# Decoder trunk with GLA, sliding-window attention and product-key experts: the gate one-hots unrolled over all tiles, one sub-key search in every query unit, two splits moved ahead of two pair subtractions

## The reference, cut to what matters

```python
def peer_ffn(h, wq, subkeys, u, v):
    K = PEER_TOPK                                        # 16
    q = (h @ wq).reshape(B, T, PEER_HEADS, 2, PEER_QDIM // 2)
    s = einsum('bthpd,pnd->bthpn', q, subkeys)           # 8 heads x 2 halves, 128 sub-keys each
    s_top, i_top = lax.top_k(s, K)
    cand = s_top[..., 0, :, None] + s_top[..., 1, None, :]
    cand_idx = i_top[..., 0, :, None] * PEER_NKEYS + i_top[..., 1, None, :]
    best, pos = lax.top_k(cand.reshape(B, T, PEER_HEADS, K * K), K)
    experts = take_along_axis(cand_idx.reshape(B, T, PEER_HEADS, K * K), pos, axis=-1)
    gates = softmax(best)
    a = einsum('td,tkd->tk', h, u[experts])              # u, v: 16384 x 1024
    return einsum('tk,tkd->td', gates * gelu(a), v[experts])
```

## Time and profile before

| | |
|---|---|
| median of three executions | 4135.0 us (4130.0 to 4140.92) |
| the profiled execution | 4135.81 us, its span 4134.0 us, mean granted PE clock 0.977 |
| PE | 3918.7 us busy (95%), 18074 matmuls |
| PE weight loads | 3171.5 us (77%) |
| DVE | 2835.7 us (69%) |
| POOL | 1833.8 us (44%) |
| ACT | 1534.9 us (37%) |

### The profile page before, as it was taken

One profiled execution on the slowest core, in us unless ns is written; L12 is line 12 of the kernel. 1 busy time (PEld: TensorE's weight loads), 2 busy tenths in 40 slices (PEclk: granted clock), 3 DMA queues, 4 the chain that ended last, 5 costly groups with the idle time before them and its releaser, 6 DMA issues.

```text
span 4134.0 us, 49995 instructions
## 1 busy us (share of the span) xinstructions
PE 3918.7 (95%) x18074; PEld 3171.5 (77%) x18074; DVE 2835.7 (69%) x4368; ACT 1534.9 (37%) x2262; POOL 1833.8 (44%) x956
## 2 busy tenths in 40 slices
PE   6899989989999999999988999899899999999999
PEld 5667767877877887888876677688687878788887
DVE  6435535798898937888764364258898978378786
ACT  3436523333333333333334364233333333333332
POOL 2322233334444447677423223334443444477772
PEclk9999999999999999999999999999999999999999
DMA  8744593333544469999857455633344445799995
GB/s 311 250 158 160 187 356 119 108 124 127 198 174 158 170 223 369 367 354 352 303 192 244 161 191 187 213 121 131 122 154 170 170 162 193 265 367 367 355 353 204
DMA packets 411796, 918.88 MB, mean 222 GB/s; under 512 B 38352, under 2 KB 176464, under 8 KB 409968
## 3 DMA queue, kind: packets, MB, share of 16 engines
q1 hardware_dynamic: 327600, 664.77, 46.4%
q0 software_dynamic: 45056, 134.38, 8.9%
q10 hardware_dynamic: 38976, 117.66, 7.3%
HBM read 794.00 MB, written 256.90 MB: 254 GB/s over the span
## 4 chain that ended last, share of the span: by engine, by line
PE 76%; issue 8%; DVE 5%; DMA 4%; POOL 4%; ACT 3%; SPq 0%; POOLq 0%; ACTq 0%; DVEq 0%
PE ps L942 13%; PE ps L943 13%; PE ps L944 13%; PE ps L957 10%; PE ps L958 10%; PE ps L959 10%; POOL w_lo L896 4%; DMA raw<-in_stream_dram 4%; PE ps L1253 2%; ACT w_hi L554 1%; PE ps L1143 1%; DVE raw L1329 1%; DMA ada_first<-in_stream_dram 0%; DVE hot_i L1686 0%; PE ps L1094 0%
## 5 line engine op out<-in xcount | busy, mean ns | idle before, releaser
L896 POOL TENSOR_TENSOR w_lo<-raw,w_hi 128x1024 fp32r<-128x1024 f32 x440 | 1124.3, 2556 | 1938.6 <-ACT w_hi L554 1938.3
L554 ACT ACTIVATE w_hi<-raw 128x1024 fp32r<-128x1024 f32 x504 | 534.0, 1060 | 1774.9 <-PE ps L944 1307.3
L942 PE MATMUL ps<-h_hi,w_hi 128*128 128x512 f32 x2880 | 1139.5, 396 | 18.1 <-POOL w_lo L896 9.6
L943 PE MATMUL ps<-h_hi,w_lo 128*128 128x512 f32 x2880 | 1131.0, 393 | 0.0
L944 PE MATMUL ps<-h_lo,w_hi 128*128 128x512 f32 x2880 | 1130.0, 392 | 0.0
L942 PEld LDWEIGHTS ps<-h_hi,w_hi 128*128 128x128 f32 x2880 | 546.0, 190 | 142.3 <-issue 17.5
L944 PEld LDWEIGHTS ps<-h_lo,w_hi 128*128 128x128 f32 x2880 | 544.0, 189 | 118.5
L943 PEld LDWEIGHTS ps<-h_hi,w_lo 128*128 128x128 f32 x2880 | 544.8, 189 | 106.3
L909 POOL DMA_INDIRECT down<-expert_down,e_row x256 | 337.0, 1316 | 220.0 <-DVE ps L1739 94.5
L1686 DVE TENSOR_TENSOR hot_i<-same_i,pick 128x1024 fp32r<-128x1024 f32 x192 | 421.2, 2194 | 0.0
L901 POOL DMA_INDIRECT acts<-expert_act,e_act x256 | 372.2, 1454 | 103.9 <-issue 77.4
(11 more groups left out here) (255 smaller groups left out, 5796.4 us busy)
## 6 DMA issues: line engine op xcount, KB each, us to landing
raw<-in_stream_dram SPq DMA_DIRECT2D x648, 512.0 KB, 3.8
expert_down<-in_stream_dram SPq DMA_DIRECT2D x256, 512.0 KB, 5.9
expert_act<-gel ACTq DMA_DIRECT2D x256, 256.0 KB, 2.0
raw_more<-in_stream_dram SPq DMA_DIRECT2D x128, 512.0 KB, 6.6
expert_gate<-gatebuf ACTq DMA_DIRECT2D x12, 4096.0 KB, 12.4
a_in<-expert_act SPq DMA_DIRECT2D x128, 384.0 KB, 6.6
g_in<-expert_gate SPq DMA_DIRECT2D x128, 384.0 KB, 8.2
ada_first<-in_stream_dram SPq DMA_DIRECT2D x3, 2048.0 KB, 20.6
```

The costliest lines, as they stand in the source:

```text
L554: return act.activation(o, i, ACT.Copy)
L896: pool.tensor_tensor(w_lo[:, s, :], raw[:, b, :], w_hi[:, s, :].bitcast(F32), ALU.subtract).then_inc(lo_ready, 1)
L942: pe.matmul(o, w_hi[:, s, w], mov_hi[:, c, :], start=c == 0, stop=False)
L943: pe.matmul(o, w_lo[:, s, w], mov_hi[:, c, :], start=False, stop=False)
```

## The change

Three edits, all in the DVE stream. First, `sub_keys` is called behind `q_lo` of every query unit from the second on, so fifteen searches lie between the units and one after them. Second, the loop over three tiles is written out as 96 groups: the one-hots read `idxT` itself in place of the copy `pick`, and `add_lower` of a tile's last three groups comes three groups later, within the next tile's; semaphore counts are constants. Third, at the start of the down stage `split_down(0)` and `split_down(1)` come ahead of `pair_lo(2)` and `pair_lo(3)`. POOL's stream, which subtracts all lower halves outside the down stage, is the same as before, and so are PE's, ACT's and SP's.

```diff
--- before.py
+++ after.py
@@ -1588,7 +1588,7 @@
                     dve.wait_ge(qhi_ready, l * 16 + n + 1)
                     tt_op(q_lo[:, n % 2, :], ps[:, ORDER[m] % 2, :], q_hi[:, n % 2, :].bitcast(F32), ALU.subtract
                           ).then_inc(col_dve, 1)
-                    if n >= 3 and (n - 3) % 4 < 3:
+                    if n:
                         sub_keys(sides)
                         sides += 1
                 for n in range(sides, 16):
@@ -1667,49 +1667,45 @@
                 dve.wait_ge(idx_ready, (l + 1) * DT)
 
                 iota4 = iota.unsqueeze(1).to_broadcast([P, 4, P])
-                with dve.Fori(0, DT) as tt:
-                    step.enter(tt, 1)
-                    step(dve.tensor_copy(pick[:], idxT[:, bass.ds(tt + 1, 1)].rearrange("p o a b -> p (o a) b")))
-
-                    def row(n, r):
-                        return pick[:, r, 4 * n:4 * n + 4].unsqueeze(2).to_broadcast([P, 4, P])
-
-                    def one_hot(n):
-
-                        dve.wait_ge(hot_used, tt * 32 + (l * DT * 32 + n + 1))
-                        tt_op(hot_j[:, n % HOT], iota4, row(n, 1), ALU.is_equal)
-                        tt_op(same_i[:, n % 2], iota4, row(n, 0), ALU.is_equal).then_inc(same_ready, 1)
-
-                    def weigh(n):
-
-                        dve.wait_ge(same_ready, tt * 32 + (l * DT * 32 + n + 1))
-                        tt_op(hot_i[:, n % HOT], same_i[:, n % 2].unsqueeze(2).to_broadcast([P, 4, 2, P]),
-                              pick[:, 2:4, 4 * n:4 * n + 4].rearrange("p a t -> p t a").unsqueeze(3).to_broadcast([P, 4, 2, P]),
-                              ALU.mult).then_inc(hot_ready, 1)
-
-                    def add_lower(n):
-
-                        half, t = n // 16, 4 * (n % 16)
-                        dve.wait_ge(gate_upper, tt * 32 + (l * DT * 32 + n + 1))
-                        both = ps[:, 4 + n % 2 * 2:6 + n % 2 * 2, :].rearrange("p a (b i) -> p (a b) i", b=4)
-                        g4 = gatebuf[:, half, :, t:t + 4]
-                        tt_op(g4, both[:, 1:8:2, :].rearrange("p t i -> p i t"), g4, ALU.add).then_inc(gate_ready, 1)
-
-                    one_hot(0)
-                    for n in range(32):
-                        if n < 31:
-                            if n:
-                                dve.wait_ge(hot_ready, tt * 32 + (l * DT * 32 + n))
-                            one_hot(n + 1)
-                        weigh(n)
-                        if n >= 3:
-                            add_lower(n - 3)
-                    for n in range(29, 32):
-                        add_lower(n)
-                    dve.wait_ge(hot_ready, tt * 32 + (l * DT * 32 + 32))
-                step.leave(DT)
+
+                def row(n, r):
+                    return idxT[:, n // 32 + 1, r, n % 32 * 4:n % 32 * 4 + 4].unsqueeze(2).to_broadcast([P, 4, P])
+
+                def one_hot(n):
+
+                    dve.wait_ge(hot_used, l * DT * 32 + n + 1)
+                    tt_op(hot_j[:, n % HOT], iota4, row(n, 1), ALU.is_equal)
+                    tt_op(same_i[:, n % 2], iota4, row(n, 0), ALU.is_equal).then_inc(same_ready, 1)
+
+                def weigh(n):
+
+                    dve.wait_ge(same_ready, l * DT * 32 + n + 1)
+                    both_parts = idxT[:, n // 32 + 1, 2:4, n % 32 * 4:n % 32 * 4 + 4].rearrange("p a t -> p t a")
+                    tt_op(hot_i[:, n % HOT], same_i[:, n % 2].unsqueeze(2).to_broadcast([P, 4, 2, P]),
+                          both_parts.unsqueeze(3).to_broadcast([P, 4, 2, P]), ALU.mult).then_inc(hot_ready, 1)
+
+                def add_lower(n):
+
+                    half, t = n // 16 % 2, 4 * (n % 16)
+                    dve.wait_ge(gate_upper, l * DT * 32 + n + 1)
+                    both = ps[:, 4 + n % 2 * 2:6 + n % 2 * 2, :].rearrange("p a (b i) -> p (a b) i", b=4)
+                    g4 = gatebuf[:, half, :, t:t + 4]
+                    tt_op(g4, both[:, 1:8:2, :].rearrange("p t i -> p i t"), g4, ALU.add).then_inc(gate_ready, 1)
+
+                one_hot(0)
+                for n in range(DT * 32):
+                    if n < DT * 32 - 1:
+                        if n:
+                            dve.wait_ge(hot_ready, l * DT * 32 + n)
+                        one_hot(n + 1)
+                    weigh(n)
+                    if n >= 3:
+                        add_lower(n - 3)
+                add_lower(DT * 32 - 3)
+                add_lower(DT * 32 - 2)
+                add_lower(DT * 32 - 1)
+                dve.wait_ge(hot_ready, (l + 1) * DT * 32)
                 pick_tile(0)
-
                 def product(j):
                     b = j % 4
                     dve.wait_ge(ag_loaded[b], 32 * (l * 16 + j // 4 + 1))
@@ -1742,10 +1738,12 @@
                 finished = x_ready if l < DEPTH - 1 else out_ready
                 for j in range(4):
                     product(j)
-                for j in range(4):
-                    pair_lo(j)
+                pair_lo(0)
+                pair_lo(1)
                 split_down(0)
+                pair_lo(2)
                 split_down(1)
+                pair_lo(3)
                 rows_n = 0
                 for n in range(NK):
                     if n + 2 < NK:
```

## The result

| | |
|---|---|
| changed kernel | 4071.16 us, median of 4 runs (4066.17 to 4073.09) |
| kernel before, on the same chip | 4133.35 us, median of 4 runs (4130.0 to 4140.92) |
| ratio after / before | 0.9845, 95% interval 0.9828 to 0.9862 |
| forecast | 4070 (4056 to 4092) |

A forecast was written before the change was run, and what follows sets the result against it. PE, busy 95% of the span, was taken as the bound, so only its idle time and slow clock could be won. 27.1 - 1 + 34.2 + 5.5 = 65.8 us off 4135.8 gives 4070, range 4056 to 4092.

The forecast's parts named there:

- Sub-key searches: Searches moved between query units: PE's 23.7 us of waits for `picked` and the slow clock behind them go, 27.1 us gross.
- one deduction: Tile 2's `picked` might come late through a stretched multiply: 0.5 us per layer, 1 us in all, taken off.
- The cover: Query units: DVE's idle time of 0.63 us per unit hides the moved searches, so they cost nothing.
- The yardstick: Tile 3's chain, transposes to end of `picked`, 21.9 us; PE asks at 22.3, leaving tile 2 0.4 us in hand.
- The upper end: Tile 2's `picked` late by 1.7 us per layer if POOL's contention stretches the multiply: 3.4 us in place of 1.
- Gate groups: Tile borders written out: waits for `hot_i` and `gatebuf`, 23.8 us, and 10.4 us of slow clock go, 34.2 in all.
- DVE as the bound inside the tiles: Rival, gate groups: border waits return inside the tiles, giving back the 34.2 us, so 4104; chance 0.09.
- Two splits: Down stage's start: first `w_lo` wait and slow clock go, 13.3 us gross; less 4.4 and 3.4, net 5.5.
- New waits: Down unit 10: PE waits for a split behind fetched rows, 1.4 us in layer 1, 3.0 in layer 2, 4.4 together.
- Half clock after the new waits: Down stage: PE's lower clock after each new wait loses 1.7 us, between 0 and 3.2; 3.4 us in all.
- DMA-bound down stage: Rival: DMA bounds the down stage and the earlier start is handed back, costing the 5.5 us: 4075 or 4076; chance 0.14.
- Overrun of the query units: Rival: searches over 0.63 us longer overrun the 15 units, 4.7 us a unit, 141 us, so 4211; chance 0.03.

The follow-up runs named there:

- e1_searches_only: Kernel before with only the first edit, a sub-key search behind q_lo of every query unit from the second on: 4113.9 us, ratio 0.9928.
- e2_straight_only: Kernel before with only the second edit, the 96 gate groups written out and reading idxT: 4102.0 us, ratio 0.989.
- e4_without_splits: Changed kernel without the third edit, so with the old order of pairs and splits: 4074.0 us, ratio 0.9832 to the kernel before.
- e7_two_more: Changed kernel with two more MAX8, results unused, behind each search between the query units: 4073.5 us, ratio 0.9836 to the kernel before.
- e6_straight_drained: Changed kernel, groups still written out, but a tile's three last add_lower ahead of the next tile's first one-hot: 4102.7 us, ratio 0.9905 to the kernel before.

## Why the forecast was right, and where it wasn't

**The size.** 4070 forecast, 4071.2 measured. The sum was made against one profiled execution of 4135.8: 65.8 off. That of the changed kernel is 62.7 off, 68.0 in the touched stages less 5.3 in the others, which the forecast put at 0. It is therefore right by its terms, within 2.2 us of their sum, and that it came within 1.2 us of the median is luck. The mean granted clock rose to 0.985, where the forecast said some 0.982.

**Sub-key searches: right, one deduction superfluous.** The cover held (0.62), ACT's exponential comes last, and the waits of 23.7 are gone. The stage gave 28.0 for 26.1 forecast: 1 us from the deduction, 1 from the clock. The forecast gave each layer 1.7 us for the half clock behind the wait, which is layer 1's row, but the same window in layer 2 is longer:

```profile
2945.14:2952.14 7.00, 7.00 (x21) 5.65 (x22) 5.69 (x8) 0.55 (x2) 0.00 (x0) 0.59 0.01 2
```

That is 5.7 us at half, 2.9 lost. (Half clock behind the last score, which the forecast left out, lost about 3 us before and after.) The 1 us taken off for a late `picked` of tile 2 was not needed, and the reason is a double count. The yardstick, tile 3's chain of 21.9 us in the kernel before, already had one stretched multiply in it. This row of the kernel before, which the forecast did not look at, shows it:

```profile
944.87 4.38 DVE L1638 TENSOR_TENSOR match<-match,topf 128x2048 f32<-128x2048 f32 x1
```

Tile 2's chain now has the same one (910.09, 4.37) and lasts the same 21.9. The stretched multiply is indeed commoner than before: of sixteen, the median was 2294 ns, and is

```profile
L1638 DVE TENSOR_TENSOR match<-match,topf x16: 2291/4366/4371, 866.1 to 3455.0; 128x2048 f32<-128x2048 f32 x16
```

What decides it is which of the two engines began first. Here are both multiplies of tile 2's chain and POOL's subtractions beside them:

```profile
902.60 2.29 DVE L1638 TENSOR_TENSOR match<-match,topf 128x2048 f32<-128x2048 f32 x1
902.97 4.19 POOL L896 TENSOR_TENSOR w_lo<-raw,w_hi 128x1024 fp32r<-128x1024 f32 x1 [3.42 <-ACT w_hi L554]
...
908.41 3.90 POOL L896 TENSOR_TENSOR w_lo<-raw,w_hi 128x1024 fp32r<-128x1024 f32 x1 [1.25 <-ACT w_hi L554]
910.09 4.37 DVE L1638 TENSOR_TENSOR match<-match,topf 128x2048 f32<-128x2048 f32 x1
```

POOL's subtraction takes 2.4 us in the median. The first multiply was there before POOL's subtraction: it keeps its 2.29, and POOL's takes 4.19. The second came while POOL's was under way: it takes 4.37. So it is in all 32 of these multiplies, before and after: the 17 that began while one of POOL's was running take 4.36 to 4.38, and the other 15 take 2.29, though POOL begins during 11 of them. The Trainium skill, GPSIMD Engine Reference, Specifications, says that POOL and DVE contend when DVE has two inputs in SBUF; the trace agrees. The upper end that the forecast drew from it, 3.4 us, was not reached, because in the chains of tiles 2 and 3 POOL's subtraction begins ahead of the second multiply only, in both layers. (In tile 1's chain it begins ahead of both, and there 16 us of cover had been counted.)

The same contention accounts for most of DVE's 37 us more with six operations fewer (4362 for 4368). `hot_i` follows the same rule: in the changed kernel the 92 that began while POOL subtracted take 3.41 to 3.43 us and the other 100 take 1.21 or 1.22. Its mean rose from 2194 to 2271 ns (15 us over 192 of them), and that of `same_i` from 980 to 1049 (13 us). Three more stretched multiplies make 6. In the gate groups this is time in which DVE would wait for PE anyway.

**Gate groups: right.** 34.2 forecast, 34.5 measured within the change, 34.4 alone. The reading of the border (drain, not branch) is shown by the drained version, and with it the size: its stages are 593.9 + 593.6, 32.5 longer. The rival, DVE as the bound inside the tiles, did not come: `hot_j` still waits for PE, 57.6 us in 91 waits.

**Two splits: right in the net, by two errors that cancel.** Gross 13.3 forecast. The stage with no wait at all lasts 534.9, the one before 542.0 and 541.4, so 13.6. New waits: 4.4 forecast, 5.9 measured; the one of layer 1 is mis-sized, 3.5 in place of 1.4 and beyond the 1 to 3 us that were to be its sign, and that of layer 2 came out at 2.4 in place of 3.0. What failed is taking one profile for where the fetched rows stand. In layer 1 POOL's first fetch starts 7.3 us after the last expert matmul (1525.31, before it was 6.3: 1554.70 against 1548.44), and the split is ready 45.6 us after it (1563.6 less 1517.98) where it was 43.7: 1.9 later, and 1.4 + 1.9 = 3.3 of the 3.5. The edit is not what moved it. In e1_searches_only and e2_straight_only, which have the old order of splits, the same distance is 45.7 and 45.8 us, in e4_without_splits 44.6, and in the five profiles with the new order and the rows at unit 7 it is 45.0 to 45.8. So the fetched rows move from one profile to the next, and the profile of the kernel before, from which the wait was worked out, had them early. Half clock after the new waits: 3.4 forecast, 2.2 measured (540.3 + 537.6 less twice 534.9 less the waits of 5.9). In layer 1 it came and in layer 2 it did not, in the 10 us behind each wait (columns as in the earlier trace rows):

```profile
1563.70:1573.70 10.00, 9.95 (x36) 8.02 (x37) 10.00 (x10) 4.40 (x5) 8.78 (x5) 0.83 1.06 392
3572.90:3582.90 10.00, 9.99 (x43) 8.14 (x44) 10.00 (x11) 5.31 (x6) 8.48 (x6) 1.00 1.05 385
```

The two errors, +1.5 and -1.2, cancel; net 5.5 forecast and 5.5 by the lengths. That the wait is caused by the rows ahead of the split is shown by moving them.

**DMA-bound down stage: refuted.** With a DMA share of 1.05 PE ran 100 us without a gap.

**Overrun of the query units: the place and the threshold right, the price wrong.** The forecast priced an overrun of 2.1 - 0.6 = 1.5 us a unit at 4.7, because it assumed that a wait in every unit keeps the clock at half. With 1.0 over, it was 14 us a layer, 1.0 a unit on average, and the clock stayed at 1.00 through the waits in the units. The window that the assumption rests on was a matter of chance too: the wait of 1.43 us ahead of the last score of layer 1 stands in 13 of the 14 profiles, and half clock follows it in four.

## What to carry to other kernels

This loop's borders cost what was drained there, and not the branch: before writing a loop out, look at which operations stand ahead of the first one that the other engine needs, and let the last ones of one iteration run into the next. When an engine's in-order stream holds both a late-arriving input's work and something that another engine needs soon, put the first behind the second; here one constant (`ROW0`) took 5.2 us off the down stages, as much as the reordering of the splits had (4.9). Before a chain is used as a yardstick with a penalty on top, look whether it has the penalty in it already. And a wait that is the small difference of two times of 40 us needs those times from more than one profile.

## What was not expected of the hardware

- Short waits repeated for 80 us (0.6 us of every 7.65) left the granted clock at 1.00. A single wait of 1.4 us is followed by 7 us at a mean of 0.54 in the kernel before and by full clock in nine other profiles. One of 3.54 is followed by 3.4 us at half, and one of 2.36 by nothing; of two waits of 2.92 at this place, in e7_two_more and e6_straight_drained, one has 3.4 us at half behind it and the other nothing. No run here tells what decides it.
- An operation beside POOL's subtraction is not slowed by a share: the multiply lasts 2.29 or 4.37 us, 2.1 more, and `hot_i` 1.22 or 3.42, 2.2 more, though the one is twice as long as the other. The multiply is stretched only where POOL's operation was there first; where the multiply was first, POOL's takes 3.65 to 4.23 us in place of 2.4.
- The down stage has two speeds at a granted clock of 1.00. Its triples of matmuls follow each other after 0.6971 us in most profiles and after 0.7000 in others, for all or nearly all of the stage: in six of the 28 stages of the fourteen profiles, in both layers of one kernel and in one layer of four. Two more stages have it for a part. It is worth 2.3 us a stage, it goes with none of the edits, and what causes it stays open.
